# A new layout of the on-chip buffers in a two-block transformer kernel in split fp32

## What is computed

```python
h = rmsnorm(x, g_mix[l])
x = x + mix(h @ w_in[l], mem_k, mem_v) @ w_out[l]          # 2 layers, then one more of the second block
a, b = jnp.split(rmsnorm(x, g_ffn[l]) @ w_up[l], 2, axis=-1)
a = sum(a_pad[:, j:j + T] * conv_w[j] for j in range(3)) + conv_b
x = x + (jax.nn.silu(a) * b) @ w_down[l]                    # 1024 -> 2 x 2816 -> 1024, three times
```

## Time and profile before

| | |
|---|---|
| median of 3 runs | 933.98 us |
| profiled execution | 936.11 us, its span 934.8 us |
| PE busy | 924.5 us, 99% of the span, 7899 matmul records |
| VectorE, ScalarE, GpSimd busy | 644.2, 493.9, 35.1 us |
| read from HBM | 158.18 MB |

### The profile page before, as it was taken

One profiled execution on the slowest core, in us unless ns is written; L12 is line 12 of the kernel. 1 busy time (PEld: TensorE's weight loads), 2 busy tenths in 40 slices (PEclk: granted clock), 3 DMA queues, 4 the chain that ended last, 5 costly groups with the idle time before them and its releaser, 6 DMA issues.

```text
span 934.8 us, 18686 instructions
## 1 busy us (share of the span) xinstructions
PE 924.5 (99%) x7899; PEld 895.7 (96%) x7899; DVE 644.2 (69%) x1182; ACT 493.9 (53%) x841; POOL 35.1 (4%) x30
## 2 busy tenths in 40 slices
PE   8999999999999999999999999999999999999998
PEld 7999999999999998789999999999977999999998
DVE  5886657776667688775787667667667576565664
ACT  6663556555446465665465545456437454444451
POOL 0000000000000000000000001000222000000000
PEclk9999999999999999999999999999999999999999
DMA  9643343464554633622544653544142255545541
GB/s 346 238 180 106 130 170 138 181 232 181 185 204 153 226 135 116 258 99 106 218 179 189 233 184 142 220 181 174 43 190 91 90 196 210 184 178 199 197 145 46
DMA packets 25570, 160.68 MB, mean 172 GB/s; under 512 B 2960, under 2 KB 4880, under 8 KB 6800
## 3 DMA queue, kind: packets, MB, share of 16 engines
q1 hardware_dynamic: 24912, 158.45, 45.9%
q10 hardware_dynamic: 576, 1.05, 0.4%
HBM read 158.18 MB, written 1.05 MB: 170 GB/s over the span
## 4 chain that ended last, share of the span: by engine, by line
PE 95%; DVE 2%; ACT 1%; DMA 1%; issue 0%; SPq 0%
PE ps L378 93%; PE ps L394 1%; DMA raw<-in_w 1%; DVE wl L1222 0%; ACT wh L2004 0%; ACT arena L2274 0%; DVE arena L1645 0%; SPq L2487 0%; DVE arena L1661 0%; DVE arena L1715 0%; ACT arena L2034 0%; DVE arena L1896 0%; DVE arena L1277 0%; ACT L2274 0%; DVE arena L1640 0%
## 5 line engine op out<-in xcount | busy, mean ns | idle before, releaser
L1222 DVE TENSOR_TENSOR wl<-raw,wh 128x1024 fp32r<-128x1024 f32 x282 | 331.0, 1222 | 139.6 <-ACT wh L2004 139.6
L378 PE MATMUL ps<-xh,wh 128*128 128x256 f32 (+1 forms) x1312 | 371.8, 283 | 1.4 <-DVE wl L1429 1.0
L378 PE MATMUL ps<-xl,wh 128*128 128x256 f32 (+1 forms) x1312 | 366.9, 280 | 0.0
L378 PE MATMUL ps<-xh,wl 128*128 128x256 f32 (+1 forms) x1312 | 366.2, 279 | 0.0
L2004 ACT CAST wh<-raw 128x1024 fp32r<-128x1024 f32 x282 | 280.8, 1047 | 133.6 <-PE ps L378 120.4
L378 PEld LDWEIGHTS ps<-xh,wh 128*128 128x128 f32 x1312 | 246.9, 188 | 5.2 <-issue 2.6
L378 PEld LDWEIGHTS ps<-xl,wh 128*128 128x128 f32 x1312 | 247.0, 188 | 0.1
L378 PEld LDWEIGHTS ps<-xh,wl 128*128 128x128 f32 x1312 | 247.0, 188 | 0.0
L378 PE MATMUL ps<-fh,wh 128*128 128x256 f32 x528 | 148.6, 281 | 0.0
L378 PE MATMUL ps<-fh,wl 128*128 128x256 f32 x528 | 148.3, 281 | 0.0
L378 PE MATMUL ps<-fl,wh 128*128 128x256 f32 x528 | 148.3, 281 | 0.0
(11 more groups left out here) (226 smaller groups left out, 963.7 us busy)
## 6 DMA issues: line engine op xcount, KB each, us to landing
raw<-in_w SPq DMA_DIRECT2D x145, 1024.0 KB, 4.8
raw<-in_w ACTq DMA_DIRECT2D x4, 256.0 KB, 5.9
xt<-in_x SPq DMA_DIRECT2D x4, 256.0 KB, 7.0
arena<-in_mem SPq DMA_DIRECT2D x1, 1024.0 KB, 8.6
out<-xt SPq DMA_DIRECT2D x8, 128.0 KB, 1.9
arena<-in_sel SPq DMA_DIRECT2D x3, 256.0 KB, 5.9
small<-in_small SPq DMA_DIRECT2D x1, 623.0 KB, 5.8
arena<-in_gmask SPq DMA_DIRECT2D x1, 512.0 KB, 9.4
```

What stands on the lines that cost most here:

```text
L378: return pe.matmul(out, lhsT, rhs, start=start, stop=stop, skip_group_check=True)
L1222: v.tensor_tensor(L[:, s], src[:, s], f32(H[:, s]), ALU.subtract).then_inc(*w_lo.up(2 * S[i] + a))
```

## The change

The buffers are declared in another order and some with other widths. xh and xl get chunks of 320 columns in place of 272 (the added ones are not used). `rst` grows to 32 columns and stands ahead of `xh`; `meta`, a gap of 16 columns and `cst` (widened to 896) stand between the others; `arena` shrinks by 4 columns and stands between `fh` and `fl`. `nrst` moves from the arena into `rst`. `gw` gets no buffer of its own but shares `wn`, and is filled at pair 7 in place of pair 5. Nothing is computed otherwise.

```diff
-    xh_, xl_ = sb("xh", 8 * TM, F32R), sb("xl", 8 * TM, F32R)
-    coh_, col_ = sb("coh", 8 * T, F32R), sb("col", 8 * T, F32R)
+    ARW, XS = 13696, 320
...
+    rst_ = sb("rst", 32)
+    xh_ = sb("xh", 8 * XS, F32R)
+    meta_ = sb("meta", 8 * NM)
+    xl_ = sb("xl", 8 * XS, F32R)
+    sb("gap", 16)
+    coh_ = sb("coh", 8 * T, F32R)
+    cst = sb("cst", 896)
+    col_ = sb("col", 8 * T, F32R)
+    fh_ = sb("fh", 4 * T, F32R)
+    arena = sb("arena", ARW)
+    fl_ = sb("fl", 4 * T, F32R)
     memkv = sb("memkv", 4 * 1024)
     small = sb("small", NSM)
-    wn_ = sb("wn", 256)
-    cst = sb("cst", NCN)
-    ARW = 13700
-    arena = sb("arena", ARW)
-    fh_, fl_ = sb("fh", 4 * T, F32R), sb("fl", 4 * T, F32R)
-    rs_, rst_ = sb("rs", TM), sb("rst", 16)
-    meta_, gw_ = sb("meta", 8 * NM), sb("gw", 256)
+    wn_, rs_ = sb("wn", 256), sb("rs", TM)
...
-    xh, xl = v3(xh_[:, :], TM), v3(xl_[:, :], TM)
+    xh, xl = v3(xh_[:, :], XS), v3(xl_[:, :], XS)
-    XFH, XFL = (lambda c: xh[:, c, :]), (lambda c: xl[:, c, :])
+    XFH, XFL = (lambda c: xh[:, c, 0:TM]), (lambda c: xl[:, c, 0:TM])
+    gw = wn
-    scB, sc8, sn, nrst = area(12), area(48), area(32), area(2)
+    scB, sc8, sn, nrst = area(12), area(48), area(32), rst_[:, 16:18]
-                if tag == "f1" and p == 5:
-                    v.memset(gw_[:, :], 0.0).then_inc(*s_gw1.up(0))
+                if tag == "f1" and p == 7:
+                    v.memset(wn_[:, :], 0.0).then_inc(*s_gw1.up(0))
```

More of the change, by code:

```diff
@@ L183, in program @@
     xt_ = sb("xt", 8 * T)
-    xh_, xl_ = sb("xh", 8 * TM, F32R), sb("xl", 8 * TM, F32R)
-    coh_, col_ = sb("coh", 8 * T, F32R), sb("col", 8 * T, F32R)
+    rst_ = sb("rst", 32)
[9 more added lines that the diff above has]
+    fl_ = sb("fl", 4 * T, F32R)
     memkv = sb("memkv", 4 * 1024)
     small = sb("small", NSM)
-    wn_ = sb("wn", 256)
-    cst = sb("cst", NCN)
-    ARW = 13700
-    arena = sb("arena", ARW)
-    fh_, fl_ = sb("fh", 4 * T, F32R), sb("fl", 4 * T, F32R)
-    rs_, rst_ = sb("rs", TM), sb("rst", 16)
-    meta_, gw_ = sb("meta", 8 * NM), sb("gw", 256)
+    wn_, rs_ = sb("wn", 256), sb("rs", TM)
     xt = v3(xt_[:, :], T)
     xs = [xt[:, c, :] for c in range(8)]
-    xh, xl = v3(xh_[:, :], TM), v3(xl_[:, :], TM)
+    xh, xl = v3(xh_[:, :], XS), v3(xl_[:, :], XS)
     coh, col = v3(coh_[:, :], T), v3(col_[:, :], T)
     meta = v3(meta_[:, :], NM)
-    gw = v3(gw_[:, :], 32)
     XH, XL = (lambda c: xh[:, c, NM:TM]), (lambda c: xl[:, c, NM:TM])
-    XFH, XFL = (lambda c: xh[:, c, :]), (lambda c: xl[:, c, :])
+    XFH, XFL = (lambda c: xh[:, c, 0:TM]), (lambda c: xl[:, c, 0:TM])
     wn = v3(wn_[:, :], 32)
+    gw = wn
     metag, mq2 = wn_[:, 0:8 * NM], wn_[:, 8 * NM:16 * NM]
```

## The result

The changed kernel takes 925.79 us (median of 6, 923.09 to 927.82) against 934.18 (6 runs, 932.99 to 936.75), ratio 0.9904 (95% interval 0.9881 to 0.9926; the quotient of the two medians is 0.9910). It is faster, by 8.4 us and not by 26.6; 907.5 was forecast, and the time lies above the range of 899 to 924.

What follows compares the result with a forecast made beforehand. PE bounds the kernel, by number of matmuls times pitch. Gains of 27.7 us, less 0.6 for re-entries, 0.6 for other engines and 0.2, plus 0.3, make 26.6: from 934.0 to 907.5 us, range 899 to 924.

Steps and rivals of the forecast that it cites:

- The pitch depends on addresses: Dense matmuls: each distance has its own settled pitch; all 6192 move to 192, the quickest seen, counted at 113.5 ns.
- takes some three matmuls to get there: Dense matmuls: after a change of distance the pitch needs about three matmuls to settle at that distance's value.
- the 27.7 forecast: Dense matmuls on x, fh/fl and coh/col: gains of 13.5, 8.7 and 5.5 us, together 27.7 us.
- Turned roles: 432 matmuls with the weight moved, distance now 64: 0.3 us gain, bounds 2.8 us gain and 0.9 loss.
- 272 columns: 192 matmuls with 272 columns, now starting at distance 128 in every chunk: 0.2 us of loss.
- The fp32 work: The other 1083 records, from arena, constants and small tables: may gain or lose 7 us, taken as 0.
- The moved fill of `gw`: Ones column and squared gain written two pairs later on DVE, into wn: same three small instructions, no effect.
- The half KB: Low parts an odd multiple of 512 bytes past high ones, new for coh/col and fh/fl: counted at nothing.
- The 0.6 for other engines: Between 15 and 55 us, where DVE has little room, shorter pitch becomes waits: 0.6 us written off.
- a PE that needs 4% less still ends last: Feed-forward stretch: with DVE busy 134.6 and ACT 101.7 of 182 us, the quicker PE still finishes last.
- The locked conflict: Rival: any constant distance locks the two reads together, x goes to 119.9 ns, 12 us slower, 946; chance 0.11.
- Half of it: Rival: only x gains fully, coh and fh settle higher or DVE's chain takes over, 921 us; chance 0.12.

Runs made afterwards that it cites:

- run 10: run 8 with 16 columns (64 bytes) put ahead of all buffers, so every address moves and all distances stay; 913.99 us.
- run 8: Changed kernel with x chunk 0 at distance 64, chunk 1 at 128, chunks 2 to 7 at 192; coh/col and fh/fl at 192; 914.21 us, ratio 0.9790.
- run 11: x chunks as in run 8 together with coh/col as in run 9; 912.74 us, ratio 0.9770 to the kernel before.
- run 2: Changed kernel with chunk 0 of xh and xl 64 bytes lower, at distance 128, the others left at 192; 917.41 us, ratio 0.9815.
- run 9: run 8 with only x chunk 0 at 64 and the rest at 192, and coh/col chunks 4 and 5 at 64 and 128; 920.66 us, ratio 0.9856.
- run 3: Changed kernel with each low part an even multiple of 512 bytes past its high part, distance 192 kept; 926.93 us.

## Why the prediction was wrong

**What bounds the kernel, and that the pitch depends on the distance:** right. Every run moved with the pitch of the dense matmuls, but for the steps of the clock and about 1 us of waits, and run 10 shows that it is the distance. That nothing hangs on the clock was not so: 3.4 us of the profile before do, by the estimate above.

**The step that failed** is the one in "The pitch depends on addresses": "So the pitch settles at a value that belongs to the distance, 113.3 at 192 and 119.9 at 0". At 192 there are two values, and what comes before decides between them. I read 113.3 from chunks that always stood behind one at 64 and one at 128, and that is what made them quick: runs 8, 10 and 11 put those two ahead again and have 113.3 from either state, nine times out of nine from the slow one; with only 128 (run 2) or only 64 (run 9) ahead a slow stretch stayed slow in 20 of 22 units. The change took the two away and kept only the 192. The rows could not show the other value at 192, since in them no chunk at 192 had anything else ahead. But the same trace had distance 0 twice: coh/col throughout, 119.9 ns, and chunk 3 of every x unit, behind a chunk at 192. Its first matmul and the one behind its six:

```profile
236.17 0.28 PE L378 MATMUL ps<-xh,wh 128*128 128x256 f32 x1
...
236.87 0.28 PE L378 MATMUL ps<-xh,wh 128*128 128x256 f32 x1
```

That is 0.70 us, and over all units of the first part 117.7 ns with single intervals from 112 to 122. So "takes some three matmuls to get there" did not hold at 0, and six matmuls behind other distances did not give the value of a constant one.

**The terms.** The two profiles have the same 7899 matmuls in the same order, so each interval from one start to the next can be set against its partner; those under 0.15 us in both are inside a stretch at the full clock. There the x matmuls with 256 columns take 2.7 us less (13.5 forecast), fh/fl 3.9 (8.7 forecast), coh/col 2.9 (5.5 forecast). All three fail by the one cause: some 4070 of these were at 117.8, and 4.5 ns each is 18.3 us, which is the 27.7 forecast less the 9.5 measured. Where a stretch was slow, x at 117.8 is even 0.7 ns worse than its old 117.1, and fh/fl only 1.2 better than 119.0.

**Small terms.** Turned roles: 1.0 us less where 0.3 was taken, within its bounds. 272 columns: 1.0 us less in all, but that is the stretch at 1.2 GHz, which fell on them in the profile before; between intervals at the full clock they lose 0.1, where I had a loss of 0.2. The fp32 work gains 0.4 us where nothing was taken. The moved fill of `gw`: nothing seen, as said. The half KB, counted at nothing: right (run 3). The 0.6 for other engines: PE waits 13 times for 7.8 us, where it was 10 times for 6.8. And "a PE that needs 4% less still ends last" failed at the end of the second, quick part: from 615.4 to 626.7 us the chain runs over VectorE and ScalarE, its longest piece there

```profile
620.18 4.63 DVE wl L1228 x4
```

with a wait of PE of 0.43 us behind it. A version that is quick throughout has VectorE closer behind PE there.

**Rivals.** The locked conflict had half of the truth at a chance of 0.11: a constant distance does let a stretch keep a bad pitch. But its price was read from distances 0 and 160, 119.9, and the slow pitch at 192 is 117.8; and it took one resting point for each distance. None of my cases had a mixture of two pitches. "Half of it" at 921 came nearest in time, for a reason that is not the one given.

**Open.** What in the start of a stretch picks the state. The first and third part were slow in both profiles of the changed kernel and in run 3, and quick in runs 2 and 9; single stretches changed between executions of one program. And why 64 followed by 128 leads to the quick pitch from both: the runs show that it does (every x unit of runs 8, 10 and 11 inside a long stretch, and the nine entries from the slow pitch), not how. Nine is few: that the order never fails is not shown, nor whether it takes this order or any two other chunks ahead would do.

## What to carry to other kernels

When TensorE streams dense matmuls back to back with a weight load for each, take the pitch from start to start, by distance between moved operand and weight modulo 256 bytes: with 256 columns of fp32r it ran from 113.3 to 119.9 ns here, 6% of the whole time. A pitch read from a mixed sequence belongs to the sequence; before giving all operands the best one's place, run a stretch in which that place stands alone. Where a stretch turns out to have two paces, a few operands put in another place can serve to bring it to the quick one. And before a spread between executions, or a difference between two profiles, is given to the kernel, sort the executions by their granted clock: here most of the spread was that.

## What was not expected of the hardware

- One stream of matmuls at one distance had two steady pitches, 113.3 and 117.8 ns, and kept one over up to 1438 matmuls (170 us) without a change.
- The state passes through chunks that have another distance: at 128 their six average 119.2 ns with the quick pitch and 118.7 with the slow one, at 64 117.7 and 118.3, and behind them it is mostly there again (20 of 22 units entered slow).
- The order 64, 128, 192 ended quick in every unit of every long stretch, also the nine times that it was entered from the slow pitch; 128 or 64 alone did so 2 times of 22. And 16 bytes off, at 176 and 208, nothing was at 113.3.
